# Seven block products: a new order of ScalarE's, VectorE's and GpSimd's work, and the output operand made on ScalarE

## The reference

```
z = (rmsnorm(x, g0) * (1 + sc1) + sh1) @ w_in           # attention q, k, v; RWKV columns; gates
x = x + gt1 * ((gateA * (attn(q, k, v) @ w_out_attn) + gateB * (rwkv(...) @ w_out_rwkv)) @ w_out)
h2 = rmsnorm(x, g1) * (1 + sc2) + sh2
u, gg = split(h2 @ w_ffn_in)                            # 1024 x 2 * 2816
x = x + gt2 * ((silu(gg) * u) @ w_ffn_out)              # 2816 x 1024
y = rmsnorm(x, g_final)
```

## Time and profile before

| | us |
|---|---|
| median of 3 runs | 1098.95 (1097.72 to 1099.9) |
| the profiled execution | 1101.9 |
| its span, first to last instruction | 1100.0 |
| TensorE matmuls busy | 1021.9 (93%) |
| VectorE busy | 575.6 (52%) |
| ScalarE busy | 439.7 (40%) |
| GpSimd busy | 377.2 (34%) |
| mean granted TensorE clock | 0.973 |

### The profile page before, as it was taken

How to read it: one execution, slowest core, us unless ns; L and a number is a source line. 1 busy time by engine, 2 the same in 40 slices (tenths; PEclk the granted TensorE clock), 3 DMA queues, 4 the chain that set the end, 5 groups by cost and what they waited for, 6 DMA issues and landing times.

```text
span 1100.0 us, 26188 instructions
## 1 busy us (share of the span) xinstructions
PE 1021.9 (93%) x10736; PEld 937.2 (85%) x10736; DVE 575.6 (52%) x1197; ACT 439.7 (40%) x959; POOL 377.2 (34%) x296
## 2 busy tenths in 40 slices
PE   5999999999998988999898998899999999999997
PEld 3899989999996766777787997889899899899997
DVE  4400000194044676666556688888888888820003
ACT  4442233353443444434232233455555554731112
POOL 2165423343316061401160343334344344034331
PEclk8999999999998999899998998999999999999999
DMA  9977665343211000020341632123224223222322
GB/s 358 365 264 247 215 220 190 98 142 129 91 42 36 17 8 21 13 81 2 121 139 41 200 96 77 39 77 113 78 76 114 77 76 102 80 79 80 87 71 82
DMA packets 118179, 122.27 MB, mean 111 GB/s; under 512 B 5397, under 2 KB 102849, under 8 KB 115657
## 3 DMA queue, kind: packets, MB, share of 16 engines
q1 hardware_dynamic: 112864, 111.86, 31.6%
q10 hardware_dynamic: 5224, 9.10, 2.5%
HBM read 108.33 MB, written 15.23 MB: 112 GB/s over the span
## 4 chain that ended last, share of the span: by engine, by line
PE 65%; DVE 21%; issue 7%; ACT 6%; ACTq 1%; POOL 1%; DVEq 1%; POOLq 0%
PE ps L1832 54%; PE ps L2429 7%; DVE a_f L1711 2%; PE ps L2183 2%; DVE a_f L1710 2%; DVE ws_lo L1700 1%; DVE ps L1695 1%; ACT ws_hi L1142 1%; DVE tmp_a L1669 1%; DVE ps L1693 1%; DVE s_sb L1457 1%; DVE tmp_a L1668 1%; DVE ff_g L1730 1%; PE ps L2083 1%; ACT rest L1167 1%
## 5 line engine op out<-in xcount | busy, mean ns | idle before, releaser
L658 POOL TENSOR_TENSOR w_lo<-w_raw,w_hi 128x2048 fp32r<-128x2048 f32 x29 | 133.8, 4613 | 300.4 <-ACT w_hi L838 281.1
L1832 PE MATMUL ps<-hh,w_hi 128*128 128x274 f32 x832 | 177.5, 296 | 2.8 <-DVE hl L1279 2.0
L1832 PE MATMUL ps<-hl,w_hi 128*128 128x274 f32 x832 | 174.1, 292 | 1.3 <-DVE al L1776 1.3
L1832 PE MATMUL ps<-hh,w_lo 128*128 128x274 f32 x832 | 174.3, 292 | 0.0
L790 POOL TENSOR_TENSOR ws_lo<-w_raw,ws_hi 128x512 fp32r<-128x512 f32 x63 | 102.8, 1644 | 146.9 <-ACT ws_hi L1142 146.9
L1832 PEld LDWEIGHTS ps<-hh,w_hi 128*128 128x128 f32 x832 | 133.0, 191 | 13.1 <-issue 11.2
L1832 PEld LDWEIGHTS ps<-hl,w_hi 128*128 128x128 f32 x832 | 133.0, 191 | 1.5 <-DVE al L1776 1.5
L1832 PEld LDWEIGHTS ps<-hh,w_lo 128*128 128x128 f32 x832 | 132.8, 191 | 0.8 <-issue 0.8
L2429 PE MATMUL ps<-th,ws_hi 128*128 128x274 f32 x336 | 99.7, 297 | 19.3 <-ACT rest L1167 19.3
L2429 PE MATMUL ps<-tl,ws_hi 128*128 128x274 f32 x336 | 97.7, 291 | 0.0
L2429 PE MATMUL ps<-th,ws_lo 128*128 128x274 f32 x336 | 97.2, 289 | 0.0
(11 more groups left out here) (424 smaller groups left out, 2305.6 us busy)
## 6 DMA issues: line engine op xcount, KB each, us to landing
w_raw<-in_w_ffn_in SPq DMA_DIRECT2D x44, 512.0 KB, 4.7
w_raw<-in_w_in SPq DMA_DIRECT2D x42, 512.0 KB, 5.0
ada_l<-in_w_ada SPq DMA_DIRECT2D x16, 1024.0 KB, 6.6
ada_w<-in_w_ada SPq DMA_DIRECT2D x8, 1024.0 KB, 13.2
w_raw<-in_w_ffn_out SPq DMA_DIRECT2D x16, 384.0 KB, 4.0
w_raw<-in_w_ffn_out SPq DMA_DIRECT2D x16, 320.0 KB, 3.4
g_d<-gst SPq DMA_DIRECT2D x16, 274.0 KB, 2.5
gring<-g_d SPq DMA_DIRECT2D x16, 274.0 KB, 3.1
```

The source lines that it names most:

```text
L658: pool.tensor_tensor(w_lo[:, s, 0:cols], w_raw[:, s, 0:cols], w_hi[:, s, 0:cols].bitcast(F32), ALU.subtract).then_inc(lo_done, 1)
L1832: return pe.matmul(out, lhsT, rhs, start=start, stop=stop)
```

## The change

- Product order on the side of VectorE's subtractions becomes 2, 4, 3, 6 (`SUMMED`).
- ScalarE makes the three operations of the output operand (`tile2`); VectorE's three go.
- GpSimd's `low` in the output projection (and unit `U_UP`) is made in four pieces of 512 columns, `token_low` in two.
- GpSimd's subtraction 0 of a unit also waits until the third of its four sums is made.
- ScalarE's order: product copy 6 of unit i moves from the end of unit i - 1 to behind the copy of product 0 in unit i; the `rest` copies of products 2 and 3 both stand ahead of product copy 2.
- VectorE's order: raw sums of i + 1, subtraction 6 of i, the up multiply and activation of i - 1 stand at the start of unit i; subtraction 3 moves behind the second up quarter.

```diff
-        PLAIN, SUMMED = (0, 1, 5), (2, 3, 4, 6)
+        PLAIN, SUMMED = (0, 1, 5), (2, 4, 3, 6)
@@ GpSimd
             def token_low(c):
-                pool.tensor_tensor(tl[:, :, c, :], tq[:, c % 2, :, :], th[:, :, c, :].bitcast(F32), ALU.subtract)\
-                    .then_inc(tl_done, 1)
+                for b in range(0, 4, 2):
+                    ins = pool.tensor_tensor(tl[:, b:b + 2, c, :], tq[:, c % 2, b:b + 2, :], th[:, b:b + 2, c, :].bitcast(F32),
+                                             ALU.subtract)
+                ins.then_inc(tl_done, 1)
+            def low_in_four(i, s):
+                pool.wait_ge(hi_done, i + 1)
+                pool.wait_ge(unit_mm, i - 1)
+                for b in range(0, UC, UC // 4):
+                    ins = pool.tensor_tensor(w_lo[:, s, b:b + UC // 4], w_raw[:, s, b:b + UC // 4],
+                                             w_hi[:, s, b:b + UC // 4].bitcast(F32), ALU.subtract)
+                ins.then_inc(lo_done, 1)
             for i in range(U_WO, U_UP + 1):
-                low(i, i % 2)
+                low_in_four(i, i % 2)
             def blocks_low(i, s):
                 for p in PLAIN:
+                    if p == 0:
+                        pool.wait_ge(wsum_done, i * NSM + (WSUM + 3 - U_ST * NSM))
@@ ScalarE
             def tile2(k):
+                a = tmp_a[:, k % 2, :]
+                act.wait_ge(pair_free, T_WO + k)
+                if k >= 2:
+                    act.wait_ge(tq_done, TQ + 4 * (k // 2))
+                act.activation(a[:, 0:T], xT[:, k, 0:T], ACT.Copy, scale=gsc[:, 1, k, 0:1])
+                act.activation(a[:, S0:W], xT[:, k, S0:W], ACT.Copy, scale=gsc[:, 1, k, 1:2])
+                act.activation(a[:, T:T + 2], mod[:, SH2 + k, :], ACT.Copy).then_inc(h_f32, 1)
...
-            for p in range(4, NPR):
+            for p in range(4, 6):
                 block_high(U_ST, U_ST % 2, p)
             def up(i, s):
                 kept(i, s, 0)
+                block_high(i, s, 6)
                 block_high(i + 1, 1 - s, 0)
                 block_high(i + 1, 1 - s, 1)
                 kept(i, s, 1)
+                kept(i, s, 2)
                 block_high(i + 1, 1 - s, 2)
-                kept(i, s, 2)
                 block_high(i + 1, 1 - s, 3)
                 kept(i, s, 3)
-                for p in range(4, NPR):
-                    block_high(i + 1, 1 - s, p)
+                block_high(i + 1, 1 - s, 4)
+                block_high(i + 1, 1 - s, 5)
                 gated_silu(i)
...
@@ VectorE
-                dve.wait_ge(pair_free, T_WO + k)
-                link(sts(a[:, 0:T], xT[:, k, 0:T], gsc[:, 1, k, 0:1], None, ALU.mult))
-                link(sts(a[:, S0:W], xT[:, k, S0:W], gsc[:, 1, k, 1:2], None, ALU.mult))
-                dve.tensor_copy(a[:, T:T + 2], mod[:, SH2 + k, :]).then_inc(h_f32, 1)
-                dve.wait_ge(h_f32, k + 1)
...
             def finish_unit(i):
+                dve.wait_ge(quad_ev, i * 4 + (QUAD + 11 - U_ST * 4))
+                tt(ff_a[:, :], ff_a[:, :], rstd2[:, :], ALU.mult).then_inc(ffa_f32, 1)
                 dve.wait_ge(ffa_f32, i + (FFA + 1 - U_ST))
                 activated(i)
-            def gate_up(i, s, sums=True):
+            def gate_up(i, s):
+                raw_sums(i + 1, 1 - s)
+                block_low(i, s, 6)
+                if isinstance(i, int) and i == U_ST:
+                    dve.wait_ge(quad_ev, QUAD + 8)
+                    activated(U_UP)
+                else:
+                    finish_unit(i - 1)
                 gate_first(i, s)
                 second_sums(i + 1, 1 - s)
                 block_low(i + 1, 1 - s, 2)
-                block_low(i + 1, 1 - s, 3)
                 up_second(i, s)
                 block_low(i + 1, 1 - s, 4)
                 up_first(i, s)
+                block_low(i + 1, 1 - s, 3)
                 gate_second(i, s)
-                block_low(i + 1, 1 - s, 6)
-                if sums:
-                    raw_sums(i + 2, s)
-                finish_unit(i)
```

More of the change, by code:

```diff
@@ L1120, in tile2 @@
             def tile2(k):
+                a = tmp_a[:, k % 2, :]
[5 more added lines that the diff above has]
+                act.activation(a[:, T:T + 2], mod[:, SH2 + k, :], ACT.Copy).then_inc(h_f32, 1)
                 act.wait_ge(h_f32, k + 1)
-                act.activation(hh[:, k, :], tmp_a[:, k % 2, :], ACT.Copy).then_inc(hh_done, 1)
+                act.activation(hh[:, k, :], a, ACT.Copy).then_inc(hh_done, 1)
                 if k >= 2:
@@ L1178, in up @@
                 kept(i, s, 1)
+                kept(i, s, 2)
                 block_high(i + 1, 1 - s, 2)
-                kept(i, s, 2)
                 block_high(i + 1, 1 - s, 3)
                 kept(i, s, 3)
-                for p in range(4, NPR):
-                    block_high(i + 1, 1 - s, p)
+                block_high(i + 1, 1 - s, 4)
+                block_high(i + 1, 1 - s, 5)
                 gated_silu(i)
             up(U_ST, U_ST % 2)
-            two_by_two(act, U_ST + 1, NST - 3, up)
-            up(U_DN - 2, (U_DN - 2) % 2)
+            two_by_two(act, U_ST + 1, NST - 2, up)
             LAST = NPR * (NST - 1)
@@ L1683, in raw_sums @@
                 if not (isinstance(i, int) and i == U_ST):
-                    dve.wait_ge(dlo_done, i * NSM + (DLO - U_ST * NSM))
+                    dve.wait_ge(dlo_done, i * NSM + (DLO - 1 - U_ST * NSM))
                 a11, a21, a22 = raw_block(s, 0, 0), raw_block(s, 1, 0), raw_block(s, 1, 1)
@@ L1691, in second_sums @@
                 s2, s3 = block_source(s, 2), block_source(s, 3)
+                if not (isinstance(i, int) and i == U_ST):
+                    dve.wait_ge(dlo_done, i * NSM + (DLO - U_ST * NSM))
                 dve.wait_ge(wsum_done, i * NSM + (WSUM + 1 - U_ST * NSM))
@@ L1714, in _ @@
             link(dve.memset(a_f[:, :, T:S0], 0.0))
-            for p in (2, 3):
-                block_low(U_ST, U_ST % 2, p)
+            block_low(U_ST, U_ST % 2, 2)
             dve.wait_ge(tile_mm, M_UP + 1)
@@ L1720, in _ @@
             tt(halves(ff_a[:, :]), pair(1), halves(rstd2[:, :]), ALU.mult).then_inc(quad_ev, 4)
-            for p in (4, 6):
+            for p in (4, 3):
                 block_low(U_ST, U_ST % 2, p)
-            raw_sums(U_ST + 1, (U_ST + 1) % 2)
-            dve.wait_ge(quad_ev, QUAD + 8)
-            activated(U_UP)
             def quarter(i, s, out, p, of, kept_):
@@ L1744, in up_first @@
                 quarter(i, s, ff_a[:, 0:H], 5, product_out(s, 5), 1)
-                dve.wait_ge(quad_ev, i * 4 + (QUAD + 11 - U_ST * 4))
-                tt(ff_a[:, :], ff_a[:, :], rstd2[:, :], ALU.mult).then_inc(ffa_f32, 1)
             def gate_second(i, s):
@@ L1763, in gate_up @@
                 up_first(i, s)
+                block_low(i + 1, 1 - s, 3)
                 gate_second(i, s)
-                block_low(i + 1, 1 - s, 6)
-                if sums:
-                    raw_sums(i + 2, s)
-                finish_unit(i)
             gate_up(U_ST, U_ST % 2)
-            two_by_two(dve, U_ST + 1, NST - 3, gate_up)
-            gate_up(U_DN - 2, U_DN % 2, False)
+            two_by_two(dve, U_ST + 1, NST - 2, gate_up)
             def act_low(c):
```

## The result

The changed kernel takes 1062.39 us (median of 4 runs, 1060.57 to 1065.03) against 1099.34 before (4 runs); ratio 0.9668, 95% interval 0.9641 to 0.9695. Forecast were 1070.4 us and a range of 1063 to 1084: right in its sign, and 0.6 us outside the range at its lower end. Two more comparisons gave 0.9683 (0.9654 to 0.9712) and 0.9668 (0.9648 to 0.9687). One run of the kernel before, slowed to 1486 us at a granted clock of 0.606, is in none of the comparisons.

The account below looks back on a forecast made before the run. It took a loop through VectorE, ScalarE and GpSimd (11.76 us a unit, 1.1 above TensorE's own) as the bound; 8.0 + 21.1 - 0.5 = 28.6 saved from 1101.9 gives 1073.3, moved by 2.95 to 1070.4 us; range 1063 to 1084.

Parts of the forecast that it names:

- Hold by GpSimd, and only of operations with all operands in SBUF: Seven-product stage: GpSimd's subtractions hold VectorE's SBUF-only operations, 1.28 for 0.24 and 0.77 for 0.44; PSUM operands not held.
- rival 4: 21 units: GpSimd in front twice a unit, at raw sums and up quarter; period 13.4, 1118 us, slower; chance 0.05.
- Output operand, 8.0 us: Before the seven-product stage: operand on ScalarE ends TensorE's 5.27 wait for squares; stage starts at 692.6 instead of 700.59.
- New loop of 10.8, taken as 10.9: 21 units under new orders: loop through VectorE and ScalarE replaces period 11.76; stage 229.8 for 250.9, 21.1 saved.
- rival 1: Seven-product stage: TensorE becomes the bound at period 10.65, stage 224.3, saved 26.6, total 1065; chance 0.22.
- Transition, 0.5 lost: Behind the 21 units: VectorE enters the last unit with subtraction 6 (0.7) and 1.5 of activation left; 0.5 given back.
- GpSimd's four pieces cost 4 x 1.28 at most and hide beside the 12.2 of a unit: Output projection before the stage: dividing GpSimd's subtraction adds no visible time; no gain from it in the sum.
- The basis: Profiled execution 1101.9 us less 28.6 gives 1073.3; it lies 2.95 above the median 1098.95, so moved to 1070.4.

Follow-up runs that it names:

- e3: Kernel before with only the added wait of GpSimd's subtraction 0 for the third sum, orders as before: 1074.19 us, ratio 0.9782.
- e4: Kernel before with one swap in ScalarE's order, the copy of product 3 into `rest` ahead of product copy 2: 1101.19 us, ratio 1.0037.
- e8: Kernel before with GpSimd's subtractions 0, 1 and 5 in two pieces of 256 columns each, no added wait: 1088.18 us, ratio 0.989.
- e12: Changed kernel without the added wait of GpSimd's subtraction 0: 1110.42 us, ratio 1.0125 to the kernel before.
- e1: Kernel before with only the output operand's three operations moved from VectorE to ScalarE, GpSimd's subtractions whole: 1088.95 us, ratio 0.9926.
- e10: Kernel before with output operand on ScalarE, added wait of subtraction 0 and GpSimd's pieces, no new orders: 1060.24 us, ratio 0.9665.
- e11: Kernel before with the added wait of subtraction 0 and GpSimd's pieces, operand left on VectorE: 1066.21 us, ratio 0.9707.
- e7: Changed kernel with one more ScalarE swap, copy of product 4 and product copy 4 ahead of product copy 3: 1064.89 us, changed kernel beside it 1064.92.
- e6: Kernel before with output operand on ScalarE and the added wait of subtraction 0, orders and whole subtractions as before: 1066.11 us, ratio 0.9699.
- e9: Kernel before with only GpSimd's pieces, `low` in four and `token_low` in two: 1090.38 us, ratio 0.9939.
- e15: Repeat, timed beside the changed kernel: kernel before with operand on ScalarE, pieces and added wait, no new orders: 1062.16 us, ratio 0.9655.

## Why the prediction was right or wrong

- *Hold by GpSimd, and only of operations with all operands in SBUF*: the hold is right (e3, e4, e8, e12), and its size of 1.04 and 0.32 at two operations too. "Only SBUF operands" is too narrow: it is the inputs that count. A raw sum reads two blocks in SBUF and writes PSUM, and in the kernel before (timelines of VectorE and GpSimd in the first unit) it took 1.79 for 0.69:
```profile
704.43 1.79 DVE L1687 TENSOR_TENSOR ps<-w_raw 128x512 f32<-128x512 f32 x1
...
702.59 4.78 POOL L790 TENSOR_TENSOR ws_lo<-w_raw,ws_hi 128x512 fp32r<-128x512 f32 x3 [7.70 <-ACT ws_hi L1142]
```
  The prediction's own working did count the raw sums as open to a hold, in the first unit and in rival 4.
- *Output operand, 8.0 us*: residual to stage measured 8.6 in the change, 7.9 alone (e1). Right. ScalarE's three operations took 0.72, 0.31 and 0.19, 1.2 together as estimated. The rule of the Trainium skill ("ScalarE: Activation LUTs", "Rules for kernel authors") that sends multiplications to VectorE would have been wrong here: the move away from VectorE, the engine being held, gave 7.9 (e1), and still 4.5 beside the pieces (e10, e11).
- *New loop of 10.8, taken as 10.9*: measured 10.89. Its parts are there: raw sums free by 0.5, the up quarter held, TensorE waiting only before product 6 (2.6 us in all by the starts of the matmuls; the view of waits shows 0.3 of it, as the rest is in pieces of 0.1). Stage 22.1 for 21.1. But I read this loop as the gain of the orders. It is their cost: with the hold alone TensorE decides (rival 1's period, by another way). I built the loop through ScalarE's copy into `rest` and product copy 4, with the held quarter as 0.2 on top; e7 shows that moving them alone changes nothing, and that the end of GpSimd's pair sets the quarter. The sum came out by another path than the one it was added up on, and that 10.9 fits so closely is in part luck.
- *Transition, 0.5 lost*: measured 0.3 gained. A small miss.
- *"GpSimd's four pieces cost 4 x 1.28 at most and hide beside the 12.2 of a unit"*: **this is the step that failed.** I asked what the pieces cost and not whom the whole had held. Ahead of the stretch that I looked at it held VectorE's merge subtraction for 4.29 us, and TensorE waited 2.37 behind that. In place of nothing this is worth 1.9 us in the changed kernel at equal clock, about 3 by the times of e6 and e10 with the lowered clock at that wait, and 7 without the other parts (e9), where the pieces shorten the operand's chain as well.
- *The basis*: sum of measured parts is 22.1 + 8.6 + 1.9 + 0.3 = 32.9; means of the pooled runs (1098.5, 67 runs; 1063.7, 14 runs) differ by 34.8. The rest of 1.9 fits the lowered clock ahead of the change (5 us less of it on the mean, at 0.36). About half of it belongs to the pieces too, by the stretch at the wait of 2.37 (2.6 us on the mean); where the other half comes from stays open. The first comparison's 37 us are 2 more, also within what such draws move a run by. My range ended at 1063, 2 us under rival 1, with no room for either: 5.2 us lay between the highest and the lowest run of e10 and e15 alone. The pooled mean, 1063.7, would lie inside the range; a term at nothing would be missing from the sum all the same.
- *Rival 4* has its kind right: take the hold from the changed kernel and GpSimd is in front twice a unit (e12). Its two places are wrong, so that the measured 13.2 lies near its 13.4 is in part luck.

## What to carry to other kernels

Where one GpSimd instruction and VectorE's SBUF-only operations overlap in a loop, first look at whose start can be moved by one wait: a two-line hold gave here the whole 25 us that the stage can gain, while the reordering around it cost 3. When a long instruction is cut in pieces, ask who was waiting for the whole, also ahead of the code that is being changed. A new order must be tried without its companion edits, since it can be the part that loses.

## What the runs showed of the hardware

- The engines meet not only through semaphores. A VectorE operation with two inputs in SBUF waits for the running GpSimd instruction's end, whether that has 2048 columns (4.29 for 0.73), 512 (1.28 for 0.24) or 256 (0.73 for 0.24), and also where its output lies in PSUM (the raw sum, 1.79 for 0.69). So does an operation with one input, a scaled or plain copy within SBUF (2.60 for 0.49 behind 1096 columns; 1.19 for 0.17 in e9 for a copy of two columns). With an input in PSUM none was held: 0.44 for 274 columns and 0.69 for 512 from 560 us on in all 17 traces, GpSimd running beside or not.
- The other way too: GpSimd's first half of e8 starts 0.04 us behind VectorE's operation and takes 1.31 for 0.74.
- Who comes first is decided by hundredths of a microsecond and repeats from unit to unit (before, VectorE's 512 columns win by 0.04 us and take 0.74; in e4, one swap away, they lose and take 1.84).
- A lowered granted clock for TensorE comes with waits of a few us, but not behind each: with the wait of 5.3 in all six traces that have it (6.8 us lowered), with that of 2.4 near 613 in six of eight (3.4 us). It also comes ahead of these, in code that is the same in all kernels: with the stretch near 613 counted in, 24 to 44 us up to the first residual operation. 1 us of it costs 0.36 us of span.
